# The first block of a two-block network as one chain of 512 tokens, or as two chains of 256

## What is computed

```python
def sandwich_ffn(x, w_gate_up, w_down, g_pre, g_post, shift, scale, gate):
    h = modulate(rms_norm(x, g_pre), shift, scale)
    return x + 0.5 * gate * rms_norm(swiglu(h, w_gate_up, w_down), g_post)

for l in range(DEPTH):                       # DEPTH = 2
    x = sandwich_ffn(x, w_ffn_gate_up[l, 0], w_ffn_down[l, 0], g[0], g[1], mx[0], mx[1], mx[2])
    ctx = sandwich_ffn(ctx, w_ffn_gate_up[l, 0], w_ffn_down[l, 0], g[0], g[1], mc[0], mc[1], mc[2])
    hx = modulate(rms_norm(x, g[2]), mx[3], mx[4])
    hc = modulate(rms_norm(ctx, g[2]), mc[3], mc[4])
    out_x, out_c = token_mix(hx, hc, w_in[l], w_out[l], na_rpb[l], w_pool[l], pool_scale[l], not last)
    x = x + mx[5] * rms_norm(out_x, g[3])
    x = sandwich_ffn(x, w_ffn_gate_up[l, 1], w_ffn_down[l, 1], g[4], g[5], mx[6], mx[7], mx[8])
    if not last:
        ctx = ctx + mc[5] * rms_norm(out_c, g[3])
        ctx = sandwich_ffn(ctx, w_ffn_gate_up[l, 1], w_ffn_down[l, 1], g[4], g[5], mc[6], mc[7], mc[8])
```

## Time and profile before

| | before |
|---|---|
| median of three runs | 3252.75 us (3252.32 to 3259.4) |
| profiled execution, span | 3252.7 us |
| TensorE busy | 3041.1 us, 93% |
| VectorE, ScalarE, GpSimd busy | 52%, 42%, 7% |
| mean granted TensorE clock | 0.960 |
| moved from and to memory | 476.80 MB, mean 147 GB/s |
| first block ends, second begins | about 1845 us |

### The profile page before, as it was taken

One profiled execution on the slowest core, in us unless ns is written; L12 is line 12 of the kernel. 1 busy time (PEld: TensorE's weight loads), 2 busy tenths in 40 slices (PEclk: granted clock), 3 DMA queues, 4 the chain that ended last, 5 costly groups with the idle time before them and its releaser, 6 DMA issues. The chain is left out here.

```text
span 3252.7 us, 52824 instructions
## 1 busy us (share of the span) xinstructions
PE 3041.1 (93%) x21680; PEld 2676.5 (82%) x21680; DVE 1679.5 (52%) x2538; ACT 1353.6 (42%) x2092; POOL 230.6 (7%) x318
## 2 busy tenths in 40 slices
PE   6999989989999899997889899998999999989998
PEld 4777858657777688876789889998799889988998
DVE  3222264553222633235655557656675687556765
ACT  3222242532222432233455455546464555454644
POOL 1111015101110000011300000000000000000000
PEclk9999989989999899998989999999899999999999
DMA  8555244135554232344245543644265446543553
GB/s 290 164 172 181 91 145 126 40 130 164 172 181 134 87 104 90 108 152 125 67 155 188 169 149 117 195 156 138 67 206 187 160 147 198 193 142 117 167 183 104
DMA packets 406475, 476.80 MB, mean 147 GB/s; under 512 B 11084, under 2 KB 383388, under 8 KB 406282
## 3 DMA queue, kind: packets, MB, share of 16 engines
q1 hardware_dynamic: 380176, 389.05, 37.2%
q0 software_dynamic: 25248, 84.71, 8.5%
q10 hardware_dynamic: 858, 0.29, 0.0%
HBM read 470.71 MB, written 4.84 MB: 146 GB/s over the span
## 5 line engine op out<-in xcount | busy, mean ns | idle before, releaser
L422 DVE TENSOR_TENSOR w_lo<-w_raw,w_hi 128x1024 fp32r<-128x1024 f32 x734 | 897.5, 1229 | 1245.3 <-ACT w_hi L419 1244.2
L430 PE MATMUL bank<-a_hi,w_hi 128*128 128x256 f32 (+1 forms) x3864 | 1243.1, 322 | 57.7 <-DVE a_lo L1434 16.4
L431 PE MATMUL bank<-a_lo,w_hi 128*128 128x256 f32 (+1 forms) x3864 | 1228.3, 318 | 0.0
L432 PE MATMUL bank<-a_hi,w_lo 128*128 128x256 f32 (+1 forms) x3864 | 1227.4, 318 | 0.0
L419 ACT ACTIVATE w_hi<-w_raw 128x1024 fp32r<-128x1024 f32 x734 | 770.5, 1056 | 969.1 <-PE bank L432 950.0
L430 PEld LDWEIGHTS bank<-a_hi,w_hi 128*128 128x128 f32 x3864 | 743.1, 192 | 133.2 <-issue 76.3
L432 PEld LDWEIGHTS bank<-a_hi,w_lo 128*128 128x128 f32 x3864 | 743.2, 192 | 50.4
L431 PEld LDWEIGHTS bank<-a_lo,w_hi 128*128 128x128 f32 x3864 | 744.0, 193 | 47.9
L430 PE MATMUL bank<-h_hi,w_hi 128*128 128x256 f32 (+1 forms) x1728 | 544.4, 315 | 0.0
L432 PE MATMUL bank<-h_hi,w_lo 128*128 128x256 f32 (+1 forms) x1728 | 539.5, 312 | 0.0
L431 PE MATMUL bank<-h_lo,w_hi 128*128 128x256 f32 (+1 forms) x1728 | 539.4, 312 | 0.0
(11 more groups left out here) (289 smaller groups left out, 2286.4 us busy)
## 6 DMA issues: line engine op xcount, KB each, us to landing
w_raw<-in_mlp_w SPq DMA_DIRECT2D x128, 1024.0 KB, 5.3
w_raw<-in_w_ffn_gate_up SPq DMA_DIRECT2D x88, 1024.0 KB, 5.2
m_raw<-in_w_mod POOLq DMA_DIRECT2D x128, 512.0 KB, 4.8
w_raw<-in_w_ffn_down SPq DMA_DIRECT2D x32, 1024.0 KB, 5.9
w_raw<-in_gla_w_in SPq DMA_DIRECT2D x24, 1024.0 KB, 5.3
w_raw<-in_w_in SPq DMA_DIRECT2D x16, 1024.0 KB, 5.9
w_raw<-in_ple_w_gate SPq DMA_DIRECT2D x16, 1024.0 KB, 5.2
w_raw<-in_w_ffn_down SPq DMA_DIRECT2D x16, 768.0 KB, 5.7
```

What stands on the lines that cost most here:

```text
L422: e.tensor_tensor(w_l, raw, w_h.bitcast(F32), ALU.subtract).then_inc(S.lo_ready.sem, 1)
L430: e.matmul(dst, hi, rhs_hi, start=start, stop=False)
L431: e.matmul(dst, hi, rhs_lo, start=False, stop=False)
L432: return e.matmul(dst, lo, rhs_hi, start=False, stop=stop)
```

## The change

Context and x become two chains of 256 columns through the same weights, so each weight block of the first block is fetched and cut once for context and once for x. Context goes first in each stage. While one stream's `gate_up` or products run, `renorm` of the other stream (post norm, residual, pre norm) is issued in steps: `next(between)` behind every slot in `gate_up`, behind every half slot in `product_halves`. `product_halves` takes the place of `gemm` for `w_in` and `w_out` of this block. A step scales one pair of tiles (two pairs with `pairs=2`, used in the `w_out` product of x in layer 0 and in the mixer of layer 1). The last ffn of layer 1, on x alone, keeps its separate norms. In `gate_up` the loop of the program is written out. Modulation pieces come every second slot in the first stream and every third later. Attention takes context's pairs first. Constants of the mixer move into the modulation buffer and into `tmp_g`, `tmp_y`. `TT_SHIFT` becomes 80. The diff is cut: of the new functions only their added lines stand here, moved left by 12 columns; what they replace is in the listing above.

```diff
-TT_SHIFT, T_SHIFT = 0, (80, 80, 80, 80, 80)
+TT_SHIFT, T_SHIFT = 80, (80, 80, 80, 80, 80)
...
+def mod_before(every):
+    at.unit += 1
+    if every and at.unit % every == 0 and at.mods < DEPTH * MOD_SLOTS:
+        mod_rows()
+        at.turn_due = at.mods % MOD_BATCH == 0
+def mod_after():
...
+def product_halves(w, first_col, units, s, evict, sums=None, between=None, order=None):
...
+    for p in range(units):
+        n, b = at.slot, bank[2 * (p % 2):2 * (p % 2) + 2]
+        col = first_col + p * SC
+        load(n, None, 0, lambda: wm[:, :, col:col + SC])
+        for m in range(2):
...
+                for k in tiles:
+                    if ready and p == 0 and m == 0 and k in ready:
+                        e.wait_ge(ready[k][0].sem, ready[k][1])
+                    mm = three(b[m][:, 0:T], cut_slot(w_hi, n)[:, k, m * P:m * P + P], cut_slot(w_lo, n)[:, k, m * P:m * P + P],
+                               a_hi[:, k, c], a_lo[:, k, c], k == tiles[0], k == tiles[-1])
+                mm.then_inc(S.slot_used.sem, 1)
+            if sums and p and m == 0:
+                sums(p - 1)
+            evict(None, p, units, lambda m: 2 * n + 1 + m, b, (m,))
+            ahead(n, None, 0, (m,))
+            if between:
+                next(between, None)
+        at.slot += 1
...
+def renorm(s, post, pre, pairs=1):
...
+    def add_pair(p):
+        if dve:
+            for k in (2 * p, 2 * p + 1):
+                e.scalar_tensor_tensor(out=z[:, k, c], in0=z[:, k, c], scalar=f_post[:, k:k + 1], in1=root,
+                                       op0=ALU.mult, op1=ALU.mult).then_inc(S.dve.sem, 1)
+            e.wait_ge(S.dve.sem, S.dve.n + 2)
+            e.tensor_tensor(xt[:, 2 * p:2 * p + 2, c], xt[:, 2 * p:2 * p + 2, c], z[:, 2 * p:2 * p + 2, c], ALU.add).then_inc(S.dve.sem, 1)
+        S.dve.n += 3
+        added[p] = S.dve.n
+        if act:
+            e.wait_ge(S.dve.sem, added[p])
+            if p >= 2:
+                e.wait_ge(S.pe.sem, summed_pair[p - 2])
+            e.activation(squares_of(p), xt[:, 2 * p:2 * p + 2, c], ACT.Square).then_inc(S.act.sem, 1)
+        S.act.n += 1
+        squared[p] = S.act.n
+    def sum_pair(p):
+        for m in range(2):
+            if pe:
+                e.wait_ge(S.act.sem, squared[p])
+                group_sums(sums, squares_of(p)[:, m, :], T, p == 0 and m == 0, p == 3 and m == 1)
...
+    inverted = root_of(summed)
+    yield
+    spread_root(inverted)
+    for p in range(4):
+        if p >= pairs and p % pairs == 0:
+            for x in range(p - pairs, p):
+                sum_pair(x)
+        add_pair(p)
+        if p % pairs == pairs - 1:
+            yield
+    for x in range(4 - pairs, 4):
+        sum_pair(x)
+    inverted = root_of(S.pe.n)
+    yield
+    spread_root(inverted)
+    if act:
+        e.wait_ge(S.mod_done.sem, S.mod_done.n)
...
+    each = 2 * pairs
+    for k0 in range(0, DK + each, each):
+        for k in range(k0 - each, k0):
+            if k >= 0:
+                if dve:
+                    e.wait_ge(S.act.sem, scaled[k])
+                    e.scalar_tensor_tensor(out=a_lo[:, k, c], in0=z[:, k, c], scalar=shift[:, k, s:s + 1],
+                                           in1=a_hi[:, k, c].bitcast(F32), op0=ALU.add, op1=ALU.subtract).then_inc(S.dve.sem, 1)
+                S.dve.n += 1
+                done[k] = (S.dve, S.dve.n)
+        for k in range(k0, min(k0 + each, DK)):
+            if dve:
+                e.scalar_tensor_tensor(out=z[:, k, c], in0=xt[:, k, c], scalar=f_pre[:, k:k + 1], in1=root,
+                                       op0=ALU.mult, op1=ALU.mult).then_inc(S.dve.sem, 1)
+            S.dve.n += 1
+            if act:
+                e.wait_ge(S.dve.sem, S.dve.n)
+                e.activation(a_hi[:, k, c], z[:, k, c], ACT.Identity, bias=shift[:, k, s:s + 1]).then_inc(S.act.sem, 1)
+            S.act.n += 1
+            scaled[k] = S.act.n
+        yield
+    at.normed[s] = done
...
+def ffn(layer, f, s, every=0, between=None):
+    if at.a_ready is None:
+        at.a_ready = at.normed[s]
+    gate_up(w_gu, s, every, between)
+    hidden_ready(FT)
+    kgs = [(k, min(DK, FT - k)) for k in range(0, FT, DK)]
+    rhs = (lambda k: (h_hi_f[:, k * T:k * T + T], h_lo_f[:, k * T:k * T + T]))
+    fetch_table(ACT.Sqrt)
+    gemm(w_d, kgs, 4, 4, rhs, to_z(s), S.act_evicted, every=every, sums=z_sums(s))
+    for _ in between or ():
+        pass
...
+def mix_in(layer, s, only_keys, between):
+    at.a_ready = at.normed[s]
+    if not only_keys:
+        product_halves(w, 0, 2, s, copy_to(qk_f[:, s * T:], TT, T, HEAD_DIM ** -0.5), between=between)
+    product_halves(w, NA_WIDTH, 2, s, copy_to(qk_f[:, 4 * TT + s * T:], TT, T), between=between)
+    if s == 0:
+        swap_partners(S.act_evicted.n)
+        between = rope_na()
+    if not only_keys:
+        product_halves(w, 3 * NA_WIDTH, 2, s, copy_to(ut[:].rearrange("p a t -> p (a t)")[:, s * T:], TT, T), between=between)
+    if s == 0:
+        for _ in between:
+            pass
+        pool_windows(T if only_x[0] else TT)
+        fetch_table(ACT.Exp)
+        between = mask_bias()
+    token_major(w, 2 * NA_WIDTH, 2, s, lambda t, x: v_na[:, 2 * s + t, x * SC:(x + 1) * SC], between, s == 1)
+    for _ in between or ():
+        pass
...
+    if not last:
+        at.a_ready = {k: (S.o_lo_done, pairs_out + k + 1) for k in range(heads)} | pooled_ready
+        product_halves(A["w_out"][layer], 0, 4, 1, to_z(1), z_sums(1), order=late)
+    at.a_ready = {k: (S.o_lo_done, pairs_out + first_x + k + 1) for k in range(heads)} | pooled_ready
     if last:
+        product_halves(A["w_out"][layer], 0, 4, 0, to_z(0), z_sums(0), order=late)
+        post_norm(layer, 3, 5, T, 1.0)
+    else:
+        steps = renorm(1, (layer, 3, 5, 1.0), (layer, 4, 6), 2)
+        product_halves(A["w_out"][layer], 0, 4, 0, to_z(0), z_sums(0), steps)
+        for _ in steps:
+            pass
...
+    first_norm()
+    yield ffn(0, 0, 1, 2)
+    yield ffn(0, 0, 0, 3, renorm(1, (0, 1, 2, 0.5), (0, 2, 3)))
+    repeat_bias(0)
+    yield mix(0, False, renorm(0, (0, 1, 2, 0.5), (0, 2, 3)))
+    yield ffn(0, 1, 1, 3, renorm(0, (0, 3, 5, 1.0), (0, 4, 6)))
+    yield ffn(0, 1, 0, 3, renorm(1, (0, 5, 8, 0.5), (1, 0, 0)))
+    yield ffn(1, 0, 1, 3, renorm(0, (0, 5, 8, 0.5), (1, 0, 0)))
+    yield ffn(1, 0, 0, 3, renorm(1, (1, 1, 2, 0.5), (1, 2, 3)))
+    repeat_bias(1)
+    yield mix(1, True, renorm(0, (1, 1, 2, 0.5), (1, 2, 3), 2))
+    pre_norm(1, 4, 6, T)
+    yield ffn(1, 1, 0)
+    post_norm(1, 5, 8, T, 0.5)
```

More of the change, by code:

```diff
@@ L375, in border, with rep @@
                         e.wait_ge(S.slot_used.sem, 2 * at.slot)
[L377 removed]
+            def rep(times, body, peel=False):
                 if times == 1 or peel:
@@ L386, in rep @@
                     body(None, start)
-                elif times and (pe or act or dve or sp or (pool and loads)):
+                elif times and (pe or act or dve or sp):
                     with e.Fori(0, times) as i:
@@ L557, in mod_vec, with gemm @@
                 return mod[:, o:o + 2 * DK].rearrange("p (k s) -> p k s", s=2)
-            def gemm(w, kgs, pairs, per, rhs, evict, by, mod_per=0, first_col=0, sums=None, between=None, after=None):
+            def gemm(w, kgs, pairs, per, rhs, evict, by, every=0, first_col=0, sums=None, between=None, after=None):
                 lag = at.lag if at.a_ready or pairs == per else (0, 0)
@@ L616, in b_ap @@
                     return [x[:, 0:width] for x in b]
-                rep(pairs // per, body, peel=ready is not None, loads=mod_per > 0)
+                rep(pairs // per, body, peel=ready is not None)
                 if sums:
@@ L759, in token_major @@
                     S.dve_evicted.n += tb
+                    if not ahead_first:
+                        ahead(nn, None, 0)
                     at.slot += 1
@@ L1338, in pool_products, with mix_loads @@
                 return products
-            def mix(layer, last):
-                n = T if last else TT
-                pre_norm(layer, 2, 3, TT)
+            def mix_loads(layer):
                 if pool:
@@ L2453, in network @@
                 next(blocks)
-                mods_done(8, 2)
                 at.rows = rows_mod
                 yield
-                for layer in range(DEPTH):
-                    last = layer == DEPTH - 1
-                    yield ffn(layer, 0, TT, 2 * (not last), 2 * (not last), 2 * last, 1 * (not last))
-                    yield mix(layer, last)
-                    if not last:
-                        yield ffn(layer, 1, TT, 2, 2, 2)
-                    else:
-                        yield ffn(layer, 1, T, 0, 0, 0)
+                first_norm()
[12 more added lines that the diff above has]
+                post_norm(1, 5, 8, T, 0.5)
                 for i in range(DEPTH_2):
```

471 lines of the change are left out of this document (257 added, 214 removed).

## The result

| | kernel before | changed kernel |
|---|---|---|
| median of the runs | 3253.9 us (4 runs, 3252.3 to 3259.4) | 3307.8 us (4 runs, 3298.7 to 3313.8) |
| ratio to before | | 1.0148, interval 1.0119 to 1.0177 |
| span of the profiled execution | 3252.7 us | 3296.9 us |

The change makes the kernel slower by 1.5% (48 us by the ratio, 53.9 us between the medians, 44.2 us between the two profiled spans; the profiled execution of the changed kernel was the fastest of its four). I had forecast slower, but 3274 us, with a range up to 3303: the sign is right, the size is less than half of what came.

The account below looks back on a forecast made before the run. Bounds: four ffn-end gaps on TensorE and VectorE's wait for GpSimd copies in the mix stages. Terms -102 + 26 + 5.4 + 18.8 + 31.2 + 25.7 + 16.4 = +21.5 us on 3252.7 gave 3274 us, range 3236 to 3303.

Parts of the forecast that it names:

- Parts that cost nothing: Items priced at zero: halved 512-column matmuls at 0.1133 us each, doubled weight fetches and cuts, the start (bounds -4 and +4).
- wrong in that step: Failure signs: wait before value products under 5 us, matmul spacing above 0.116, or modulation pieces waited for.
- The gaps: At the ends of ffns: four TensorE gaps, together 97.2 us, and 2.4 us of slow restart go; term -102.
- Sums and spreads: In the matmul stream: 4.6 us per renorm, five in ffns plus 3 for waits +26; doubled z sums +5.4.
- Stream ends: Eight streams each end in a TensorE wait, six of 2.4 us and two of 2.1: +18.8.
- First mix stage: First product to VectorE's first attention operation: 92.1 us before, 123.3 after, +31.2, with 21.2 us for the copies.
- my sign: In the mix stages: VectorE waits on copies over 14 us, TensorE on ScalarE's squares 2 to 5 us at a time.
- Second mix stage: First product to VectorE's first attention operation: 80.5 us before, 106.2 after, +25.7, with 18.1 us for the copies.
- The output product: First layer's x output product carrying context's renorm: idle 11.2, sums 4.2, clock 1, together +16.4 us.
- Hidden chains (B): Helper engines' waits in mix stages and output product fall within two blocks cut ahead: 3218, half 3246 us; chance 0.25.
- Late fetches (C): Single-buffered modulation pieces arrive late, each of 17 in the first stream delaying TensorE 2 us: +34, 3308 us; chance 0.13.
- Cheap sums (D): TensorE's sums cost only their own issue, 18 us less, copies land 3 us sooner twice: 3250 us; chance 0.12.

Follow-up runs that it names:

- the mix edit: Changed kernel with the mask added during x's query and key products and the rotation behind both value slots' cuts, in both mix stages: 3299.0 us, ratio 1.0136.

## Why the prediction was wrong

- **The step that failed** is the first of "Parts that cost nothing": "the 5328 wide matmuls cost nothing by being halved". The spacing cost 22.9 us in the first block. That this is the whole distance between 21.5 forecast and 44.2 measured is chance: the other misses, of up to 7 us each way, cancel. The row was read rightly, 0.1133 us over 54 steps; it was taken for all. Other 256-column stretches of the same trace run at 0.118 us (3382 steps of 0.116 to 0.119 us behind the first block, beside 6078 below), and one grouped look at them would have given 0.1149 and, over 10,656 halves, a term of 17 us, which brings the forecast to 3291. That trace also has 501 steps of 256 columns at 0.120 us in the first block, where the shift was 0. My own bound for "wrong in that step" was a spacing of 0.116, which a mean of 0.1156 passes: over ten thousand matmuls two per cent of a spacing is 25 us.
- **The gaps** went as forecast (-89.6 against -87.8), and no transfer was late.
- **Sums and spreads** in the ffns: 24.4 measured, 30 forecast; a fifth less. **Stream ends** were priced at 2.4 us; five of them cost 1.5 us more in slow clock.
- **First mix stage:** the mechanism was right, each wait where it was named, released by the cut behind the rotation. Its size was not: 8.1 us of idle, not 16, since VectorE got on 12.5 us behind the first copy's issue (539.80 to 552.25, rows below) and not 21.2. That number was copied from the trace of before. GpSimd's queue pauses once among the eight copies: here for 3.67 us behind the second, in the first mix of before for 9.54 us behind the sixth (the last two go out at 528.98), and so in the second mix of both. It is no scatter: with shift 0, with the mix edit and without the sums the first mix has it behind the second too. What puts the pause there no run tested. VectorE waited for the copies for 7.8 and 11.8 us, where my sign said over 14, and TensorE for squares for 0.5 to 1.3 us at a time, where it said 2 to 5.

GpSimd's timeline in the changed kernel, the copies and its own first operation behind their landing, then VectorE's:

```profile
539.80 1.07 POOL L1298 DMA_DIRECT2D prob<-qk  x2 [54.21 <-ACT qk L735]
544.54 3.16 POOL L1298 DMA_DIRECT2D prob<-qk  x6 [3.67 <-issue]
552.27 0.33 POOL L1465 MEMSET m_raw<- 128x272 f32 x1 [4.57 <-DMA prob<-qk]
...
552.25 1.22 DVE L1428 TENSOR_TENSOR probT<-qk,m_raw 128x1024 f32<-128x1024 f32 x1 [7.81 <-DMA prob<-qk]
```

- **Second mix stage:** 12.2 us idle ahead of x's values, 13 forecast; 4.8 ahead of x's first product, where I had 7. The piece is right to 0.4 us, but by luck: 37.5 us to x's first product where my terms make 40.6, 25.1 from there to the first copy where they make 22.2, 16.4 for the copies where I had 18.1.
- **The output product** came out 4.2 us too long: waits of 2.9 and 5.0 us for VectorE's pair sums, of which I had 5.3 in one.
- **Not in the sum at all:** 1.7 and 1.1 us more in the two attentions, 2.0 more in the second output product with its norms, the start 6.2 us earlier (the bound was 4; the some 5 us of first wait and slow clock in the ffns give most of it back), some 3 us of spacing behind the block.
- **Rivals.** Hidden chains (B): no, each wait was there. Late fetches (C): no. Cheap sums (D): no, 24.4 of the 30 us in the ffns came; leaving six of eight sums out took only 2 us off the insertions, as those left cost more each (a spread of the root 1.37 us for 1.06), and the time did not come near 3250.
- **Two slips** in the prediction change nothing here: six ends of 2.4 and two of 2.1 make 18.6 and not 18.8, and the first block ends at about 1845 us, not 1645.

## What to carry to other kernels

A spacing read from one stretch is a sample: before it multiplies ten thousand matmuls, take the mean over every stretch of that shape, and a bound from the slowest. A change of tile width and the placement of operands go together, and each width has to be timed at several placements: of the two shifts at which both widths were run, 0 was the better for 512 columns and 80 for 256. A serial gap of 24 us, hidden in steps, comes back as insertions, stream ends and late neighbours; here four gaps of 100.8 us in all went, and 145 us of other time came in their place, 23 of them spacing.

## What the hardware showed that I had not expected

- TensorE's spacing at full clock depends on where the stationary operand lies: 512 columns 0.227 us at shift 0 and 0.233 at 80; 256 columns 0.1195 at 0, 0.1156 at 80, others between. The Trainium skill's page "TensorE: Matmul & The Clock Gate", section "Back-to-back issue gap", gives for a matmul by itself one gap for each width (262 cycles for 256 columns, an estimated 0.109 us at 2.4 GHz), says that among weight loads both operations set the spacing, and does not speak of placement; no step between 256-column products of the first block was under 0.112 us in any of these traces, and the measurement decides.
- At shift 80 the spacing has two values, 0.113 and 0.118 us, and mostly keeps one from one interruption (a modulation piece, a sum, a slow stretch) to the next. All 19 switches in the changed kernel's first ffn stood right behind an inserted group or a slow stretch; from 1326 to 1888 us all but two did, and these two (1454.69 and 1822.99 us) stood at the first product of the hidden values, where the moving operand is another tile. What picks the value is open; shorter insertions did not help (the run without the sums had more of the slower).
- A wait of 1.4 to 1.7 us at a stream's end was followed by 14 to 16 matmuls at the lower clock in five of eight places, and by none in the others. It isn't the place: with the mix edit it was five again, three of them others (255.6, 463.1 and 1111.4 us), and without the sums two.
- Leaving work out of TensorE's queue gained nothing when it changed which spacing followed: a difference under 6 us between two versions of this kernel can be that alone.
